# Sample scores of four sequences in four column tiles, and prompt scores in pairs of 64 rows

## What is computed

```python
def mla_attend(q_lat, q_rope, q_pos, kv_row, k_pos):
    ckv, krope = kv_row[..., :MLA_KV_LORA], kv_row[..., MLA_KV_LORA:]
    s = jnp.einsum('bthc,bkc->bhtk', q_lat, ckv) + jnp.einsum('bthr,bkr->bhtk', q_rope, krope)
    p = masked_softmax(s.astype(jnp.float32) * MLA_SCALE, k_pos[None, :] <= q_pos[:, None])
    return jnp.einsum('bhtk,bkc->bthc', p.astype(ckv.dtype), ckv)
...
    s = jnp.einsum('btghd,bgtnpd->bghtnp', q_rot, kv_s[..., 0, :]).astype(jnp.float32) * NSA_SCALE
...
    o_sel = jnp.einsum('bghtnp,bgtnpd->btghd', p.astype(dt), kv_s[..., 1, :])
    s = jnp.einsum('btghd,bkgd->bghtk', q_rot, win_kv[:, :, 0]).astype(jnp.float32) * NSA_SCALE
...
    o_win = jnp.einsum('bghtk,bkgd->btghd', p.astype(dt), win_kv[:, :, 1])
```

## Time and profile before

| | us |
|---|---|
| median of the runs (lowest, highest) | 675.97 (671.38, 680.39) |
| span of the profiled execution, first to last instruction | 675.0 |
| PE busy in it | 609.6 |
| DVE, ACT, POOL busy in it | 286.9, 214.3, 93.7 |
| sample attention and sparse prompt attention | 285 to 530.6 |
| latent prompt attention and output | 530.6 to 675 |

### The profile page before, as it was taken

The page is one execution under the profiler, slowest core; times in us unless marked ns, Lnnn a source line. Parts: engine busy times, 40 slices in busy tenths (PEclk is TensorE's granted clock), DMA queues, the critical chain, the costliest instruction groups (busy, mean ns, idle before and its releaser), DMA issues. The chain is left out here.

```text
span 675.0 us, 10193 instructions
## 1 busy us (share of the span) xinstructions
PE 609.6 (90%) x3482; PEld 375.2 (56%) x3482; DVE 286.9 (43%) x758; ACT 214.3 (32%) x614; POOL 93.7 (14%) x175
## 2 busy tenths in 40 slices
PE   6889998978897999879999899999999898999995
PEld 3554554555566865554446366666566765465642
DVE  0122202263658455653345334445444345255335
ACT  1330102241324221242343243445245345053310
POOL 0114531110100320420010001021003121000000
PEclk9889997989897989959999989999999998999999
DMA  8916563368407512223302105032401701010101
GB/s 307 263 47 144 106 155 51 47 87 118 100 1 236 212 26 74 74 74 110 109 18 70 57 1 188 1 111 79 125 2 62 289 2 40 1 62 1 63 0 62
DMA packets 42381, 60.34 MB, mean 89 GB/s; under 512 B 8986, under 2 KB 34074, under 8 KB 41722
## 3 DMA queue, kind: packets, MB, share of 16 engines
q1 hardware_dynamic: 42330, 59.69, 32.3%
HBM read 55.43 MB, written 8.41 MB: 95 GB/s over the span
## 5 line engine op out<-in xcount | busy, mean ns | idle before, releaser
L828 PE MATMUL psum<-wring,bufA 128*128 128x512 f32 (+2 forms) x384 | 159.2, 570 | 2.0 <-DMA wring<-in_w_in 2.0
L828 PEld LDWEIGHTS psum<-wring,bufA 128*128 128x128 f32 x384 | 74.9, 200 | 72.8 <-issue 67.4
L1392 ACT ACTIVATE wring<-wring,small 128x128 f32<-128x128 f32 (+3 forms) x96 | 53.9, 561 | 160.4 <-DVE small L1675 160.0
L1675 DVE CUSTOM_DVE_ANT_0 wring<-psum,const 128x128 f32<-128x128 f32 (+3 forms) x96 | 46.6, 486 | 86.5 <-PE psum L1050 75.1
L803 PE MATMUL psum<-const,ring 128*128 128x128 f32 (+2 forms) x360 | 52.2, 281 | 24.7 <-ACT mid L590 11.8
L803 PEld LDWEIGHTS psum<-const,ring 128*128 128x128 f32 (+2 forms) x360 | 37.9, 138 | 38.6 <-ACT mid L590 13.7
L1278 PE MATMUL psum<-ring,comp 128*128 128x512 f32 x128 | 56.5, 595 | 1.5 <-issue 1.5
L803 PE MATMUL psum<-const,wring 128*128 128x128 f32 x272 | 49.6, 280 | 6.8 <-ACT wring L1471 3.9
L803 PEld LDWEIGHTS psum<-const,wring 128*128 128x128 f32 x272 | 34.2, 143 | 33.6 <-issue 18.5
L1050 PE MATMUL psum<-mid,qrT 128*128 128x128 f32 (+3 forms) x128 | 50.1, 475 | 2.2 <-DVE small L1669 2.2
L1081 PE MATMUL psum<-kv,wring 128*128 128x64 f32 x320 | 43.8, 268 | 1.0 <-DVE rtmp L1703 0.8
(11 more groups left out here) (227 smaller groups left out, 811.3 us busy)
## 6 DMA issues: line engine op xcount, KB each, us to landing
wring<-in_w_in SPq DMA_DIRECT2D x4, 2048.0 KB, 8.6
ring<-in_cache_cmp_kv SPq DMA_DIRECT2D x64, 128.0 KB
ring<-in_cache_mla SPq DMA_DIRECT2D x64, 80.0 KB, 1.9
ring<-in_cache_sel_kv SPq DMA_DIRECT2D x40, 128.0 KB, 2.1
ring<-in_state_win_kv SPq DMA_DIRECT2D x8, 512.0 KB, 5.4
ring<-in_w_o SPq DMA_DIRECT2D x1, 4096.0 KB, 13.7
out_s_win<-in_state_win_kv SPq DMA_DIRECT2D x1, 4064.0 KB
wring<-in_cache_sel_kv SPq DMA_DIRECT2D x24, 128.0 KB, 2.1
```

The source lines that it names most:

```text
L828: ins = pe.matmul(bank[:, 0:w], xT[:, c, t * P:(t + 1) * P], wr[:, b % 2, c, 0:w], start=(c == 0), stop=(c == KC - 1))
L1392: ins = act.activation(Pp[:, n % 4, 0:w], Pp[:, n % 4, 0:w], ACT.Exp, bias=nmp[:, k, h:h + 1], scale=-1.0, accum_out=lp[:, k, h:h + 1])
L1675: ins = dve.tensor_tensor_reduce(Pp[:, n % 4, 0:w], bank[:, 0:w], mask, -(MLA_SCALE if kind == "pmla" else NSA_SCALE), CLAMP, ALU.add, ALU ...
```

## The change

It does five things.

1. The keys of four sequences, 512 of each, are transposed before their score (steps keys, and rkeys for the rotary rows of mla), into kt, which now holds four sequences. One score step per half of the keys then issues four products of 32 query columns, into the four groups of 32 partitions of one bank; for mla one product of 128 rows by 128 columns adds the rotary part of all four sequences, from krp (32 rows of each sequence) and a block-diagonal qrope. qrope is set to zero by POOL's memory set and filled by eight copies on DVE, which wait for it (bd_zero). The rotary rows of the new tokens go to krnew by four DVE copies. The minimum is taken per half (min), and least combines them.
2. A psel or pwin score reads 64 rows of qrT and of selKT or winKT. The heads are ordered so that units follow each other on the upper and the lower 64 rows. padK and POOL's steps pad are gone.
3. The prompt list goes by pairs: scores m and m+1, then pturn and pvalue of two earlier units. The lags are 4 and 6 in place of 3 and 5, Pp holds eight units, PTp moves to another buffer.
4. zrecip of the last projection now stands before wuk and qlat; qup of the first tile stands before qh at the end of the woven stretch.
5. The first keys of mla 0 (half 0, all four sequences) are transposed during the projections.

```diff
--- before.py
+++ after.py
-UNITS = ([(i, kind, h) for i in range(PT) for kind in KINDS[:3] for h in range(G if kind == "pcmp" else H)]
+HEADS = [g * HG + hh for hh in range(HG) for g in range(G)]
+UNITS = ([(i, kind, h) for i in range(PT) for kind in KINDS[:3] for h in (range(G) if kind == "pcmp" else HEADS)]
...
-T_LAG, V_LAG = 3, 5
+T_LAG, V_LAG = 4, 6
+PBUF = 8
...
-    cmp += [([("pad", 0)], .5), ([("pad", 1)], .5)]
-
-    cmp += [([("keys", *ITEMS[0], b, part)], 1) for b in range(2) for part in range(2)]
+    cmp += [([(k, *ITEMS[0], 0, two)], 1) for k in ("keys", "rkeys") for two in range(2)]
...
-    s = [([("qhead",)], 1), ([("wuk", 0)], 1), ([("wuk", 1)], 1), ([("qlat",)], 1.5), ([("zrecip", *seq[-1])], .5)]
+    s = [([("qhead",)], 1), ([("zrecip", *seq[-1])], .5), ([("wuk", 0)], 1), ([("wuk", 1)], 1), ([("qlat",)], 1.5)]
...
+    def keys_of(x, half):
+
+        kinds = ("keys", "rkeys") if x[0] == "mla" else ("keys",)
+        return [([(k, *x, half, two)], 1.3) for k in kinds for two in range(2)]
 
...
+        body.append(([("min", *x, 0)], 0))
+        if BANKS_OF[x[0]] == 2:
+            body += keys_of(x, 1)
         if last:
             body.append(([("pv", *last)], 2))
-        body += [([("keys", *x, 2)], 1.5), ([("keys", *x, 3)], 1.5), ([("score", *x, 2)], 1), ([("new", *x)], .5),
-                 ([("score", *x, 3)], 1), ([("min", *x)], 1.5)]
-        body += [([("keys", *nxt, 0)] if nxt else [], 1.5), ([("exp", *x)], 1.5),
...
-            body.insert(8, ([("kup", 2 * g)], .6))
-            body.insert(10, ([("kup", 2 * g + 1)], .6))
+            body += [([("kup", 2 * g)], .6), ([("kup", 2 * g + 1)], .6)]
+        if BANKS_OF[x[0]] == 2:
+            body += [([("score", *x, 1)], 1), ([("min", *x, 1)], 0)]
         if last and last[0] != "sel":
...
+            body.append(([("omla",)], 1))
+        body += [([("new", *x)], .5), ([("least", *x)], .5)]
+        ahead = keys_of(nxt, 0) if nxt else []
+        body += ahead[:1] + [([], .5), ([("exp", *x)], 1)] + ahead[1:] + [([("norm", *x)], 1.5)]
...
 
-    p = [(slot(m), cost(m)) for m in range(N_NSA)]
+    def pair(m):
+
+        a, b = slot(m), slot(m + 1)
+        return a[:1] + b[:1] + a[1:] + b[1:]
+
...
-        p.insert(N_NSA // 2 + 18 + 4 * t, ([("vup", t)], .6))
-    p.insert(N_NSA, ([("qup", 0)], 1))
+        p.insert(N_NSA // 4 + 9 + 3 * t, ([("vup", t)], .6))
+    p.insert(N_NSA // 2 + PT, ([("qup", 0)], 1))
...
 
-            def turn_keys(kind, g, b, part):
-
-                if part == 0 and kind == "mla":
-                    pe.wait_ge(m_land[g * GB + b], 16 * PAGES)
...
-                    u = T.at("keys", kind, g, b, part, j=j % 2)
+            def turn_keys(rope, kind, g, half, two):
+
+                for b in (2 * two, 2 * two + 1):
+                    if half == 0 and not rope:
+                        if kind == "mla":
+                            pe.wait_ge(m_land[g * GB + b], 16 * PAGES)
+                        else:
+                            what = (kind, g, b if kind == "sel" else b // 2)
+                            pe.wait_ge(r_land[SLOT_OF[what]], ring_landed(what))
+                    src = source(kind, g, b)
...
+                    u = T.at("rkeys" if rope else "keys", kind, g, half, two, j=b % 2)
                     bank = claim(T, u)
                     for k in range(4):
-                        page = src[:, 4 * (j % 2) + k, :]
+                        page = src[:, 4 * half + k, :]
                         out = bank[:, k * P:(k + 1) * P]
-                        if kind != "mla":
-                            ins = turn(out, page[:, 0:G * HD])
-                        elif j < 2:
-                            ins = turn(out, page[:, 0:KVL])
+                        if rope:
+                            ins = turn(out[0:ROPE], page[:, KVL:ROW])
                         else:
-                            ins = turn(out[0:ROPE], page[:, KVL:ROW])
+                            ins = turn(out, page[:, 0:P])
                     ins.then_inc(T.full[u % T.n], 1)
...
 
-            def score(kind, g, b):
-
...
-                        ins = pe.matmul(out, qrope[0:ROPE, rc], krp[:, b % 2, keys], start=False, stop=True)
-                    else:
-                        ins = pe.matmul(out, qrbd[:, rc], kt[:, b % 2, keys], start=True, stop=True)
-                    if b == GB - 1:
-                        ins.then_inc(A.full[u % A.n], 1)
+            def score(kind, g, half):
+
+                for step in ("keys", "rkeys") if kind == "mla" else ("keys",):
+                    for two in range(2):
+                        for j in range(2):
+                            wait_copied(pe, T, T.at(step, kind, g, half, two, j=j))
+                u = A.at("score", kind, g, half)
+                bank = claim(A, u)
+                q = qlatT if kind == "mla" else qrbd
+                for b in range(GB):
+                    ins = pe.matmul(bank[b * RB:(b + 1) * RB, :], q[:, g * P + b * RB:g * P + (b + 1) * RB],
+                                    kt[:, b, :], start=True, stop=True)
+                if kind == "mla":
+                    ins = pe.matmul(bank, qrope[:, g * P:(g + 1) * P], krp, start=False, stop=True,
+                                    skip_group_check=True)
+                ins.then_inc(A.full[u % A.n], 1)
...
+                        wait_copied(pe, T, T.at("post", B_WINGATE, NT - 1))
                     g, hh = h // HG, h % HG
-
-                    ins = pe.matmul(bank[:, 0:keys], qrT3[:, hh, q], padK[:, int(kind == "pwin"), g, 0:keys],
-                                    start=True, stop=True)
+                    s, kT = slice(g * HD, (g + 1) * HD), selKT if kind == "psel" else winKT
+                    ins = pe.matmul(bank[:, 0:keys], qrT3[s, hh, q], kT[s, 0:keys], start=True, stop=True)
...
                     dve.tensor_copy(ckvT[:, c0:c0 + r], bank[:, 2 * r:3 * r])
+                    if t == ST:
+                        for b in range(GB):
+                            dve.tensor_copy(krnew[b * ROPE:(b + 1) * ROPE, :], bank[NOPE:QH, 3 * r:4 * r])
...
                     bank = arrive(T, u)[:, 0:H * NS_TOK]
                     dve.tensor_copy(qhT, bank[0:NOPE, :])
-                    for p0 in (0, NOPE):
-                        ins = dve.tensor_copy(qrope[p0:p0 + ROPE, :].rearrange("p (t h) -> p h t", h=H),
-                                              bank[NOPE:QH, :].rearrange("p (h t) -> p h t", h=H))
+                    dve.wait_ge(bd_zero, 1)
+                    for b in range(DEC_B):
+                        p0, t0 = b % GB * ROPE, b * DEC_T
+                        ins = dve.tensor_copy(
+                            qrope[p0:p0 + ROPE, b * RB:(b + 1) * RB].rearrange("p (t h) -> p h t", h=H),
+                            bank[NOPE:QH, :].rearrange("p (h t) -> p h t", h=H)[:, :, t0:t0 + DEC_T])
...
                 if step[0] == "zrecip" and step[1:] != (B_ZNSA, NT - 1):
                     silu(*step[1:])
-                if step[0] == "pad":
-
-                    j = step[1]
-                    wait_full(pool, B, B.at("hid", NT - 1, 0))
-                    ok(pool.memset(padK[:, j], 0.0))
-                    wait_copied(pool, T, T.at("post", B_WINGATE, NT - 1))
-                    for g in range(G):
-                        s = slice(g * HD, (g + 1) * HD)
-                        ins = pool.tensor_copy(padK[s, j, g, :], (selKT, winKT)[j][s, 0:SEQ])
-                    ins.then_inc(pad_ready, 1)
...
 
             wait_full(pool, A, A.at("proj", B_ZNSA, NT - 1))
-            ok(pool.memset(bufA[:, 0:2 * SR], 0.0))
+            pool.memset(bufA[:, 0:3 * SR], 0.0).then_inc(bd_zero, 1)
+            pool.wait_ge(bd_zero, 1)
```

More of the change, by code:

```diff
@@ L159 @@
 BANKS_OF = {k: n // 4 for k, n in PAGES_OF.items()}
-KEYS_T = {"mla": 4, "sel": 2, "win": 1}
 OUT_AT = {0: 11, 1: 17, 2: 24, 3: 33}
@@ L318, in t_uses @@
         return 2 if a[0] == B_Q else 1
[L319 to L320 removed]
+    if kind in ("keys", "rkeys"):
+        return 2
     if kind == "probs":
@@ L1359, in block_out, with keys_out @@
                     act.activation(gate3[0:r, t, :], src[:, KVW - c0:], ACT.Exp, scale=-1.0).then_inc(free, 1)
[L1361 to L1369 removed]
+            def keys_out(rope, kind, g, half, two):
+                u, b = T.at("rkeys" if rope else "keys", kind, g, half, two), 2 * two
+                bank = arrive(T, u)
+                if rope:
+                    ins = act.copy(krp[b * ROPE:(b + 1) * ROPE, :], bank[0:ROPE, :])
+                else:
+                    ins = act.copy(kt[:, b, :], bank)
+                ins.then_inc(T.free[u % T.n], 1)
             def probs_out(kind, g, part):
```

130 lines of the change are left out of this document (49 added, 81 removed).

## The result

The changed kernel takes 687.05 us (682.29 to 693.40), the kernel before 678.18 in the same comparison. The ratio is 1.016, interval 1.011 to 1.021: slower, by 1 to 2%. I had forecast 660, with 643 to 677 as the range. The span of the profiled execution is 684.9 us, where the sum gave 659.3. (All ratios here leave out executions that took over 1.5% longer than the fastest of the same kernel.)

A forecast was written before the change was run, and what follows sets the result against it. PE's own work was taken to bound the kernel nearly everywhere. Savings of 39.9 and 15 us against added waits and clock loss summed to −15.7: span 659.3, time 660 us, range 643 to 677.

The forecast's parts named there:

- Sample scores and pairs: On PE, four sample-score products side by side save 39.9 us; prompt scores two at a time on separate row halves save 15.
- Both seams: Waits at qhead's copies and reciprocal before qlat cost +4.3 us; POOL's rotation before qh, ahead of the latent stretch, costs +3.
- the pages: PE waits for SP's page fetches: +11.4 us at sel 0, +9 at sel 1, +2 at the second window.
- the loop: Path from score over DVE and ACT to the two transposition banks: PE's waits grow from 14.0 to 20 us, +6.
- the first seam: Before qlat, copies wait for POOL's memory set and the reciprocal precedes the first psel minima: +4.3 us, ends 0 and 6.
- Pages of sel 1: After pv of sel 0, PE reaches sequence 3's keys before its pages land: +9 us, ends 5 and 14.
- In the tail the longer lags change little: 0, ends −3 and +2: In the latent stretch, lags 4 and 6 were taken to add 0 us, between −3 and +2.
- The clock: +3.5, ends 0 and 8: PE's granted clock: one more slow stretch, 1.7 us lost, behind each of two long page waits; +3.5 us in all.
- The slower rival: Clock stays at 1.2 GHz from first sample score to pv of mla 0, mostly short transpositions and waits: 688 us; chance 0.08.
- Theory 2: Stated with the follow-ups: thin work (half-height products, column tiles, transpositions) lowers PE's clock, whatever PE waits for.
- Theory 1: Stated with the follow-ups: PE's clock falls behind its waits, so each wait costs itself and the slow clock behind it.

The follow-up runs named there:

- experiment 2: Changed kernel plus products with unread results, issued on PE where it otherwise waits for pages and at the start of the sample scores: 686.87 us, ratio 1.017.
- experiment 4: Changed kernel with heads in their old order 0 to 7, so both scores of a pair use the same 64 rows: 703.54 us, ratio 1.042.
- experiment 1: Changed kernel, but SP loads page numbers into registers before its wait, so pages are issued sooner: 662.31 us, ratio 0.981.
- experiment 6: Kernel with page numbers loaded ahead, plus ACT taking a pair's exponentials when the next pair's scores are due, in the woven stretch: 648.98 us, ratio 0.959.
- experiment 7: Kernel with page numbers loaded ahead, plus POOL's memory set before the last gates and the reciprocal behind the first four psel minima: 666.43 us, ratio 0.985.
- experiment 11: Changed kernel with lags 3 and 5 restored for the latent prompt units, nothing else: 673.97 us, ratio 1.000.
- experiment 8: Kernel with page numbers loaded ahead, plus four products with unread results in the wait for POOL's rotation before the first latent queries: 672.26 us, ratio 0.984.

## Why the prediction was wrong

Held against the milestones that the prediction names: qlat 299.8 (299.6 forecast), 0.2 late; end of pv of mla 0 369.9 (367), 2.7 more; first latent score 529.5 (514), 12.6 more; the end another 10.1. Together these are the 25.6 us by which the sum missed.

By terms, PE from the start of qlat to the first latent score, before and after:

```profile
295.15:530.56 235.41, 221.44 (x1437) 135.16 (x1438) 103.12 (x368) 92.74 (x279) 20.93 (x24) 0.97 0.25 76
```

```profile
299.84:529.47 229.63, 187.36 (x1397) 128.53 (x1397) 105.56 (x366) 88.32 (x270) 20.27 (x23) 0.86 0.26 81
```

PE's time without work grew by 28.3 us, where the waits of my sum made 31.4. Its work at the lower level grew from 11.8 to 48.6 us, and half of that difference is 18.4, where I had 3.5. The rest of its work fell by 52.5, where I had 54.9. This makes 14.2 us more than my sum had up to there, nearly all of it the clock. The latent stretch adds 11.0, of them 6.2 by the clock and 4.3 by waits. The clock thus has 21 of the 25.6 us. This is an account of where PE's time went, not of what could be had back: of a slow clock ahead of a landing nothing comes back (experiment 2).

- **Sample scores and pairs: right.** Four products side by side take 1.00; a pair of 512 columns takes 1.06, and 1.92 with the halves undone (experiment 4). The pair of 512 columns costs 0.19 more than one product, where I had charged 0.10. The Trainium skill ("TensorEngine Tiling (Array Packing)", Key Properties) says that changing the tiling mode drains TensorE; the row agrees in sign, and no run here isolates the change of shape.
- **Both seams, the pages, the loop: right in place and about in size**, and the pages, the loop and the first seam were each taken away by an edit of their own (experiments 1, 6 and 7). Pages of sel 1 cost 4.8 instead of 9: the slow clock ahead of their landing, which I had not forecast, brought PE to its wait later.
- **"In the tail the longer lags change little: 0, ends −3 and +2": wrong.** The tail, which is the latent stretch, takes 11.0 us more than before, and the old lags alone give 10.2 back (experiment 11). I had looked at the order, not at where ACT and DVE would be late there.
- **"The clock: +3.5, ends 0 and 8": the term that failed most.** I counted one stretch of 3.4 us more behind each of two waits, and nothing anywhere else. The rows give 69.3 us of work at the lower level instead of 17.7, 25.8 us at most, 6 of them in the tail. The two long stretches at the waits for pages were 17.1 and 20.4 us long. Only the first came behind the start of a wait, and it lasted 9.4 us behind the landing; the second began 9.4 us ahead of its wait, which no step of mine had.
- **The slower rival had the time, 688, but not the place.** It wanted the lower level from the first sample score to pv of mla 0, with transpositions as the reason. There the clock was up for most of the way (0.88 on the mean from qlat to the end of pv of mla 0); the two long stretches that are new came later. Its time was met by other terms, so that is luck. The row that I set against it is weaker than I had it, too: from 328 to 345 us only 7.0 of PE's 14.5 us of work were transpositions.

What starts a low stretch stays open. Theory 2 in its plain form, thin work whatever PE waits for, does not fit experiments 1, 2 and 8, where earlier pages or filling kept the clock up with the same thin work. Theory 1 does not fit all either: the stretch of experiment 7 and the second one of the changed kernel began while PE was busy, and in experiment 4 the waits shrank while the work at the lower level grew. That waits are the only cause is not shown, and a mixture of both was not tested.

## What to carry to other kernels

When an edit cuts the work of the engine that bounds a kernel, list what its work had covered and look at the granted clock around each wait that comes out: here taking waits for pages from 15.0 to 1.5 us gave 21 in that stretch. A slow clock ahead of an arrival that sets the time was free here; behind it, it was not, so take the wait away rather than fill it. Lags and tables of slots that were set for one stretch are to be changed in that stretch alone.

## What was not expected of the hardware

A transfer whose page number is read just before it costs SP 1.07 us; with the number already in a register, 0.50 (17.05 and 8.06 for 16). In the latent stretch 4.3 us of waits more went with 5.9 us of the same products at a lower clock (experiment 11). The clock stood at its lower level for 23.9 us in which PE worked for 22.97 (experiment 7).
